# Four layer norms: three tiles by token halves instead of two, three more weight slots, subtraction on VectorE, scale on ScalarE

## Chip, cores and metric

One core of one Trainium2 chip. The metric is device time in microseconds (us) of one execution of the whole program; lower is better.

## What is computed

Two transformer blocks on 512 tokens of 1024 channels, in float32. The first has RMS norms, two kinds of attention and a feed-forward part. The second is run for two layers, and the change is all in it:

```python
def layernorm(x, g, b):
    mu = jnp.mean(x, axis=-1, keepdims=True)
    var = jnp.mean(jnp.square(x - mu), axis=-1, keepdims=True)
    return (x - mu) * lax.rsqrt(var + LN_EPS) * g + b

def hybrid_layer(x, ...):
    fq, fk, fv, f_logit, rq, rk, rv, rg = split(x @ w_in)
    fox_out = fox_attention(fq, fk, fv, log_f)      # 8 heads, causal softmax
    ret_out = silu(rg) * groupnorm(retention(...))
    mix = concat(fox_out, ret_out) @ w_out
    x = layernorm(ALPHA * x + mix, ln1_g, ln1_b)
    ff = square(relu(x @ w_ff1)) @ w_ff2            # 1024 -> 4096 -> 1024
    return layernorm(ALPHA * x + ff, ln2_g, ln2_b)
```

So there are four layer norms: after the mix and after the feed-forward part of each layer. Three are followed by more products ("inner" norms), the fourth by the output.

## The kernel before

Activations lie transposed: channels on the 128 partitions, eight tiles `H[:, j, :]` of 128x512, a column per token. Products are made in full precision out of three passes: activations and weights are each split into a high and a low part of a reduced type (`Phi`/`Plo` or `Qhi`/`Qlo`, and `wh`/`wl`), and `product` issues hi·hi, lo·hi and hi·lo (L267, L269, L270). A `gemm` makes one output tile of 128 channels: 8 products, so 24 matmuls of 512 columns, and then an evacuation out of PSUM.

**Weights.** A slab of 1 MB (or two transfers of 512 KB) is loaded by the SP queue into one of two buffers `stage` (`load_slab`). `prepare` takes the next piece, half a slab, which is what one gemm needs: ScalarE copies the high part (L239), VectorE subtracts it for the low part (L240), both 128x1024, into one of four slots `wh`/`wl` in a ring. Splitting a slab's second piece frees the buffer and issues the next load. `piece(ahead)` hands out the next piece, after it has seen to it that pieces are split `ahead` of it.

**Order.** Every engine has one queue, in the order in which this Python code calls `PE.op`, `V.op` (VectorE), `A.op` (ScalarE), `G.op` (GpSimd) and `SP.op`. An operation waits by semaphores for the ones that it is given, and all behind it in its queue wait with it. Work that is to run under the gemms is a generator in `background`. `tick()`, called after each product, adds `pace[0]` to a counter and does one background step for each whole one. The softmax heads of the attention (`softmax_heads`) are such work: for 8 heads of 4 rows the scores, the reduce (L621), the exponential (L630), the reciprocal (L635), the scaling (L640), transposes on TensorE (L647), the copy and split of what they give (L652, L653) and the product with the values (L662). They run under the gemms for queries, keys and rotary parts, at a pace of 0.46.

**A layer norm.** `Norm.tile(j)` is called once a tile j of `H` is added up. It keeps a running sum in `accq` (L1050), has an estimated centre `cB` made after tile 1, and then sums squares of deviations from that centre: subtract (L1066), square on ScalarE (L1074), add (L1082). That is done for tiles 0 to 5, whole tiles of 512 tokens. Tiles 6 and 7 are made by `last_pair`, by halves of 256 tokens (`A_`, `B_`): both tiles for half A, then both for half B. While TensorE makes half B, the mean of half A (`mean`: a matmul with ones, copied to `muB`, L1092 to L1094) and its scale (`scale`: L1104, then logarithm and exponential, L1108 and L1109) come in between. `mean` also issues the subtraction of `muB` from all eight tiles of the half, two on VectorE and six on GpSimd (L1100). Per tile follow on VectorE the multiplication by the gain and by `rB` (`gained`, L1113), on ScalarE the bias (L1119) and the copy to `Phi` (L1122), and on VectorE the low part `Plo` (L1123). With these the first two products of what comes next (`head`) start, again first half A, then half B. In an inner norm `prepare(G)` gives one weight split to GpSimd.

In the last norm of the program there is no next product. `out_half` stores the tiles by DMA as they come.

Of the kernel before, what the change touches and what calls it, by code (L numbers as in the profile page):

```python
# [93 lines left out]
def build(nc, xT, w_in, gate_up, w_bm, w_bg, w_out, w_up, w_down, w_in2, w_out2, w_ff1, w_ff2,  # L94
          consts, params, out, vrev, cneg):
    ctx = ExitStack()
    with ctx:
# [15 lines left out]
        wl = [at(f"wl{i}", 32 + 4 * i, [128, 1024], F32R) for i in range(4)]  # L113
        Phi, Plo = at("Phi", 48, [128, 8, S], F32R), at("Plo", 64, [128, 8, S], F32R)
# [97 lines left out]
        w_tok, w_free = {}, [None] * 4  # L212
        state = {"slab": 0, "prep": 0, "use": 0, "bank": 0}
# [10 lines left out]
        def prepare(low=V):  # L224
# [3 lines left out]
            state["prep"] += 1  # L228
            n, part, (k0, k1, c0, c1), last = pieces[i]
# [4 lines left out]
            if m <= 16:  # L234
                both = wh[i % 4][:, 0:8 * (32 + m)].rearrange("p (k c) -> p k c", k=8)
                hi, lo = both[:, :, 0:m], both[:, :, 32:32 + m]
            else:
                hi, lo = (w[i % 4][:, 0:size].rearrange("p (k c) -> p k c", k=k1 - k0) for w in (wh, wl))
            t_hi = A.op(lambda e: e.activation(hi, src, ACT.Copy), st_landed[n], w_free[i % 4], sem=s_whi)  # L239
            t_lo = low.op(lambda e: e.tensor_tensor(lo, src, hi.bitcast(F32), ALU.subtract),  # L240
                          st_landed[n], t_hi, w_free[i % 4], sem=s_wlo if low is V else None)
            if m <= 16:
                t_lo = [t_lo, V.op(lambda e: e.memset(both[:, :, m:32].bitcast(F32), 0.0), w_free[i % 4], sem=s_wlo)]
# [34 lines left out]
        def gemm(x, nk, evac):  # L278
# [11 lines left out]
            w_free[i % 4] = x.free = t  # L290

        def gemm_thin(x, dst, wait):
# [12 lines left out]
            w_free[i % 4] = x.free = t  # L305
# [4 lines left out]
        def gemm_pair(x, evac0, evac1, order=range(8), between=None):  # L310

            two = [(piece(), next_bank()) for _ in range(2)]
            for n, k in enumerate(order):
                for (i, w), b in two:
                    t = product(banks[b][:, :], w, k, slice(0, 128), x, k, n == 0, n == 7, free[b] if n == 0 else None)
                    if n == 7:
                        w_free[i % 4] = t
# [8 lines left out]
        def gemm_tok(x, evac):  # L326

            for q in range(4):
# [17 lines left out]
                w_free[i % 4] = t  # L346
# [629 lines left out]

        def hidden(scale_tok=None):
# [18 lines left out]
        def ff(up, first):  # L996


            for g in range(4):
                for j in range(2 if g == 0 else 0, 8):  # L1000
                    gemm(P, 8, lambda o, t, j=j: up(j, o, t))
                for j in range(6 if g == 3 else 8):
                    def ev(o, t, j=j, g=g):
# [6 lines left out]
                        return t_h[j]  # L1010
                    gemm(Q, 8, ev)
# [5 lines left out]
        for j in ff(up1, None):  # L1017
# [17 lines left out]
        class Norm:  # L1035
# [9 lines left out]
            def tile(self, j):  # L1045
# [9 lines left out]
                for k in {2: (0,), 3: (1, 2), 4: (3, 4), 5: (5,)}.get(j, ()):  # L1055
# [503 lines left out]
```

How the kernel before makes its waits and increments, by code:

```python
    def run(self, eng):  # L85
        for need, fn, s, inc in self.ops:
            for w, v in need:
                eng.wait_ge(w.h, v)
            ins = fn(eng)
            if s:
                ins.then_inc(s.h, inc)
# [1400 lines left out]
        @block.sync  # L1492
        def _(e):
            SP.run(e)
            e.wait_ge(s_out.h, s_out.n)
```

## Time and profile before

| | before |
|---|---|
| runs | 2193.04, 2193.93, 2195.63 us, median 2193.93 |
| the profiled execution | 2193.07 us |
| its span in the trace | 2191.1 us |
| mean granted TensorE clock | 0.986 of full |
| TensorE matmul (PE) busy | 2089.3 us (95%) |
| TensorE weight load (PEld) | 1702.0 us (78%) |
| VectorE (DVE) | 1120.9 us (51%) |
| ScalarE (ACT) | 924.7 us (42%) |
| GpSimd (POOL) | 189.8 us (9%) |

The profile is of one execution. PEld runs beside PE. Matmuls are pipelined: the duration of one in the trace runs from its start to its end through the array, so their starts lie closer than their durations.

### The profile page before, as it was taken

What the parts mean: (1) busy time and instruction counts of PE and PEld (TensorE: products, weight loads), DVE (VectorE), ACT (ScalarE), POOL (GpSimd) and SP (SyncE); (2) the same over time, 40 slices, a digit from 0 to 9 for tenths busy, and PEclk for the clock granted to TensorE, in tenths of its full rate; (3) what the DMA queues carried; (4) which work ended last, traced back from release to release, by engine and by line L of the source; (5) the groups of instructions that cost most, each with busy time, mean ns of one, the idle gap of its engine ahead of it and who ended that gap; (6) DMA issues with size and microseconds to landing.
All of it is one profiled execution on the core that took longest, in us unless ns stands there. A gap on an engine that the chain in (4) does not pass through costs nothing.

```text
span 2191.1 us, 24398 instructions
## 1 busy us (share of the span) xinstructions
PE 2089.3 (95%) x9592; PEld 1702.0 (78%) x9592; DVE 1120.9 (51%) x1744; ACT 924.7 (42%) x1497; POOL 189.8 (9%) x258
## 2 busy tenths in 40 slices
PE   6999999999999999999998999998999998999997
PEld 5778767888888888777787888887777677888886
DVE  4555554655433434567466333337667465333336
ACT  4565222524422323455546243343565346243343
POOL 0000000000000000243011000002353010000001
PEclk9999999999999999999999999999999999999998
DMA  6332211323223232633221223232533231323231
GB/s 210 87 92 74 77 58 58 135 92 101 96 95 98 96 96 78 183 92 97 101 96 59 96 96 96 96 96 59 164 106 92 92 96 58 96 96 96 96 96 58
DMA packets 201517, 211.36 MB, mean 96 GB/s; under 512 B 7803, under 2 KB 181115, under 8 KB 201404
## 3 DMA queue, kind: packets, MB, share of 16 engines
q1 hardware_dynamic: 194544, 194.13, 27.8%
q0 software_dynamic: 6352, 15.24, 2.7%
q8 instruction: 76, 1.25, 0.2%
q10 hardware_dynamic: 508, 0.43, 0.1%
q14 instruction: 37, 0.30, 0.0%
HBM read 194.55 MB, written 8.95 MB: 93 GB/s over the span
## 4 chain that ended last, share of the span: by engine, by line
PE 82%; DVE 8%; ACT 7%; issue 2%; DMA 0%; POOL 0%; DVEq 0%; ACTq 0%; SPq 0%
PE ps L267 23%; PE ps L270 23%; PE ps L269 23%; PE ps L335 2%; PE ps L340 2%; PE ps L338 2%; PE ps L662 1%; PE ps L647 1%; ACT H L1119 1%; PE ps L1412 1%; DVE wl L240 1%; ACT wh L239 1%; PE ps L1398 1%; ACT Phi L1122 1%; DVE d L1066 1%
## 5 line engine op out<-in xcount | busy, mean ns | idle before, releaser
L267 PE MATMUL ps<-Phi,wh 128*128 128x512 f32 (+1 forms) x1520 | 610.5, 402 | 37.3 <-DVE Plo L1123 20.4
L270 PE MATMUL ps<-Phi,wl 128*128 128x512 f32 (+1 forms) x1520 | 587.6, 387 | 0.0
L269 PE MATMUL ps<-Plo,wh 128*128 128x512 f32 (+1 forms) x1520 | 587.4, 386 | 0.0
L239 ACT ACTIVATE wh<-stage 128x1024 fp32r<-128x1024 f32 (+1 forms) x339 | 351.6, 1043 | 289.8 <-PE ps L270 278.7
L240 DVE TENSOR_TENSOR wl<-stage,wh 128x1024 fp32r<-128x1024 f32 x333 | 406.4, 1222 | 70.3 <-ACT wh L239 62.9
L267 PE MATMUL ps<-Qhi,wh 128*128 128x512 f32 (+1 forms) x1056 | 402.7, 381 | 0.8 <-DVE Qlo L400 0.8
L270 PE MATMUL ps<-Qhi,wl 128*128 128x512 f32 (+1 forms) x1056 | 399.2, 378 | 0.0
L269 PE MATMUL ps<-Qlo,wh 128*128 128x512 f32 (+1 forms) x1056 | 399.2, 378 | 0.0
L267 PEld LDWEIGHTS ps<-Phi,wh 128*128 128x128 f32 x1520 | 290.5, 191 | 104.5 <-issue 43.7
L270 PEld LDWEIGHTS ps<-Phi,wl 128*128 128x128 f32 x1520 | 290.0, 191 | 58.0
L269 PEld LDWEIGHTS ps<-Plo,wh 128*128 128x128 f32 x1520 | 290.9, 191 | 53.6 <-issue 4.1
L267 PEld LDWEIGHTS ps<-Qhi,wh 128*128 128x128 f32 x1056 | 200.9, 190 | 38.8 <-ACT Qhi L399 1.6
L269 PEld LDWEIGHTS ps<-Qlo,wh 128*128 128x128 f32 x1056 | 200.8, 190 | 37.4 <-issue 1.0
L270 PEld LDWEIGHTS ps<-Qhi,wl 128*128 128x128 f32 x1056 | 200.7, 190 | 36.4
L400 DVE TENSOR_TENSOR Qlo<-f,Qhi 128x512 fp32r<-128x512 f32 x96 | 66.5, 693 | 253.3 <-ACT Qhi L399 253.3
L1009 DVE TENSOR_TENSOR H<-H,ps 128x512 f32<-128x512 f32 x74 | 50.8, 687 | 221.1 <-PE ps L270 221.1
L985 ACT ACTIVATE rl<-ps 128x512 f32<-128x512 f32 x64 | 38.2, 598 | 194.7 <-PE ps L270 194.7
L990 ACT ACTIVATE f<-rl 128x512 f32<-128x512 f32 x96 | 60.7, 632 | 116.6 <-DVE rl L987 114.5
L335 PE MATMUL ps<-wh,Phi 128*128 128x512 f32 x224 | 92.5, 413 | 1.9 <-DVE x_rb L1351 1.9
L340 PE MATMUL ps<-wl,Phi 128*128 128x512 f32 x224 | 89.1, 398 | 0.0
L338 PE MATMUL ps<-wh,Plo 128*128 128x512 f32 x224 | 88.8, 396 | 0.0
L1310 POOL TENSOR_SCALAR x_bi<-x_Cb,stat 128x128 f32<-128x128 f32 (+1 forms) x64 | 69.3, 1083 | 116.1 <-DVE stat L621 110.1
(287 smaller groups left out, 1899.9 us busy)
## 6 DMA issues: line engine op xcount, KB each, us to landing
stage<-in_w_ff SPq DMA_DIRECT2D x64, 1024.0 KB, 5.3
stage<-in_w_in SPq DMA_DIRECT2D x39, 1024.0 KB, 5.1
stage<-in_w_up SPq DMA_DIRECT2D x16, 1024.0 KB, 5.2
stage<-in_w_down SPq DMA_DIRECT2D x16, 1024.0 KB, 5.2
stage<-in_w_in SPq DMA_DIRECT2D x30, 512.0 KB, 5.0
stage<-in_w_out SPq DMA_DIRECT2D x12, 1024.0 KB, 5.3
stage<-in_w_bg SPq DMA_DIRECT2D x4, 1024.0 KB, 5.5
vrev<-H SPq DMA_DIRECT2D x2, 2048.0 KB, 12.6
```

The costliest lines, as they stand in the source:

```text
L239: t_hi = A.op(lambda e: e.activation(hi, src, ACT.Copy), st_landed[n], w_free[i % 4], sem=s_whi)
L240: t_lo = low.op(lambda e: e.tensor_tensor(lo, src, hi.bitcast(F32), ALU.subtract), st_landed[n], t_hi, w_free[i % 4], sem=s_wlo if low is ...
L267: PE.op(lambda e: e.matmul(o, hi[:, k, c], x.hi[:, kx, tok], start=first, stop=False), t_hi, t_x or x.t[kx], list(waits), signal=False)
L269: PE.op(lambda e: e.matmul(o, hi[:, k, c], x.lo[:, kx, tok], start=False, stop=False), signal=False)
L270: return PE.op(lambda e: e.matmul(o, lo[:, k, c], x.hi[:, kx, tok], start=False, stop=last), t_lo, sem=s_wpe, signal=last)
L335: PE.op(lambda e, k=k, kk=kk, sl=sl, o=o, hi=hi: e.matmul(o, x.hi[:, kk, sl], hi[:, k, :], start=(kk == 0), stop=False), t_hi, x.t[kk], fr ...
L338: PE.op(lambda e, k=k, kk=kk, sl=sl, o=o, hi=hi: e.matmul(o, x.lo[:, kk, sl], hi[:, k, :], start=False, stop=False), signal=False)
L340: t = PE.op(lambda e, k=k, kk=kk, sl=sl, o=o, lo=lo: e.matmul(o, x.hi[:, kk, sl], lo[:, k, :], start=False, stop=(kk == 7)), t_lo, sem=s_w ...
L400: t2 = V.op(lambda e: e.tensor_tensor(lo, src, hi.bitcast(F32), ALU.subtract), t1, t_src, x.free, after)
L990: t = A.op(lambda e: e.activation(f[:, :], r[:, :], ACT.Square), t_r, f_free[j % 2])
L1009: t_h[j] = V.op(lambda e: e.tensor_tensor(H[:, j, :], H[:, j, :], o, ALU.add), t, t_h[j])
L1310: t = G.op(lambda e: e.tensor_scalar(bi[n % 2][:, 0:w], Cb[h % 2][:, 0:w], stat[:, 96 + 8 * i + h:97 + 8 * i + h], None, ALU.add), t_Cb[h] ...
```

## The change

- `last_pair` becomes `last_three`: tiles 5, 6 and 7 are made by token halves, and the next stage begins with three products by halves instead of two.
- Three more weight slots (`wxh`/`wxl`), used by `prepare(extra, room)`. `ahead_of(j)` and a further `prepare(2, ...)` split five pieces around tile 4. The extra slots lie in room that is free only then. `prepare` no longer goes to GpSimd.
- The subtraction of the mean (`minus`) is on VectorE for all eight tiles. VectorE multiplies by `rB` only (`times`); ScalarE's activation, which added the bias, now multiplies by the gain too. The order in which mean, scale and these steps are put between the products is new.
- The input stage of each layer makes query and key pair 1 before the attention's heads begin. The pieces of `w_in` are reordered for that, and the pace under which the heads run goes from 0.46 to 0.52.
- `ff` starts at tile 3 and leaves three tiles over.

```diff
+        for i, off in enumerate((54, 62, 84)):
+            wh.append(at(f"wxh{i}", 111 + off, [128, 1024], F32R))
+            wl.append(at(f"wxl{i}", 115 + off, [128, 1024], F32R))
...
             pair_cols(w_in2[L], 0)
+            pair_cols(w_in2[L], 1)
             cols(w_in2[L], 1536, 1544)
             values(w_in2[L], 1024, 1536)
-            pair_cols(w_in2[L], 1)
...
-        def prepare(low=V):
+        def prepare(extra=None, room=None):
...
+            if extra is None:
+                u = state["ring"] % 4
+                state["ring"] += 1
+            else:
+                u = 4 + extra
+                w_free[u] = room
+            slot[i] = u
...
+        def ahead_of(j):
+            if j >= 2:
+                prepare()
+            if j == 4:
+                prepare()
+                prepare(0, done(PE, V, A))
+                prepare(1, w_free[4])
...
-        def ff(up, first):
+        def ff(up, first, begun, whole):
...
-                for j in range(2 if g == 0 else 0, 8):
+                for j in range(begun if g == 0 else 0, 8):
...
-                for j in range(6 if g == 3 else 8):
+                for j in range(whole if g == 3 else 8):
...
+                    if g == 3 and whole == 5:
+                        ahead_of(j)
                     gemm(Q, 8, ev)
...
-                for k in {2: (0,), 3: (1, 2), 4: (3, 4), 5: (5,)}.get(j, ()):
+                for k in {2: (0,), 3: (1, 2), 4: (3, 4)}.get(j, ()):
...
-                for k in range(8):
-                    q = V if k < 2 else G
-                    self.d[k] = q.op(lambda e, k=k: e.tensor_tensor(d8[:, k, sl], H[:, k, sl], muB[:, sl],
-                                                                    ALU.subtract), t_m, t_h[k], self.d[k])
+            def minus(self, *ks):
+                sl = self.sl
+                for k in ks:
+                    self.y[k] = V.op(lambda e, k=k: e.tensor_tensor(d8[:, k, sl], H[:, k, sl], muB[:, sl], ALU.subtract),
+                                     self.t_m, t_h[k], self.n.d[k])
...
+            def times(self, *ks):
+                sl = self.sl
+                for k in ks:
+                    t = V.op(lambda e, k=k: e.tensor_tensor(d8[:, k, sl], d8[:, k, sl], rB[:, sl], ALU.mult),
+                             self.r, self.y[k])
+                    g, b = (prm[:, v + k:v + k + 1] for v in (self.vg, self.vb))
+                    self.fin[k] = A.op(lambda e, k=k, g=g, b=b: e.activation(H[:, k, sl], d8[:, k, sl], ACT.Identity,
+                                                                             bias=b, scale=g), t)
...
+            for p in range(3):
+                part(p, 0, range(8))
+            norm.add()
+            part(0, 1, range(3))
+            A_.mean()
+            A_.minus(0, 1, 2, 3)
+            part(0, 1, (3, 4))
+            A_.scale()
+            A_.minus(4, 5, 6, 7)
+            part(0, 1, (5, 6, 7))
+            A_.times(0, 1)
+            A_.lows(0)
+            part(1, 1, range(8))
+            for k in range(2, 5):
+                A_.times(k)
+                A_.lows(k - 1)
+            part(2, 1, range(8))
+            norm.add()
...
             if L == 0:
                 gemm_pair(P, ev_fq(0), ev_fk(0))
+                gemm(P, 8, ev_fq(1))
             else:
-                last_pair(norm, None, V_LN2G, V_LN2B, (ev_fq(0), ev_fk(0)))
+                last_three(norm, None, V_LN2G, V_LN2B, (ev_fq(0), ev_fk(0), ev_fq(1)))
                 t_ph = done(V, A, PE)
+            gemm(P, 8, ev_fk(1))
...
             gemm_tok(P, ev_fv)
-            pace[0] = 0.46
+            pace[0] = 0.52
...
-            for ev in (ev_fq(1), ev_fk(1), ev_r(0), ev_fq(2), ev_fk(2), ev_r(1), ev_r(2), ev_fq(3), ev_fk(3),
+            for ev in (ev_r(0), ev_fq(2), ev_fk(2), ev_r(1), ev_r(2), ev_fq(3), ev_fk(3),
                        ev_r(3), ev_r(4), ev_r(5), ev_r(6), ev_r(7)):
...
-            for j in range(2, 6):
+            for j in range(2, 5):
+                ahead_of(j)
                 gemm(Q, 8, ev_out(j))
-                prepare()
+                if j == 4:
+                    prepare(2, done(PE, V, A))
                 norm.tile(j)
...
-            for j in ff(up, alpha):
+            for j in ff(up, alpha, 3, 5):
```

VectorE's queue at the start of the first inner norm's stage, before. L1454 adds a whole tile into `H` (tiles 3, 4 and 5 here), L240 is a weight split, L1142 adds a half tile:

```order
L1454 SCALAR_TENSOR_TENSOR H<-H,ps 128x512
L240 TENSOR_TENSOR wl_55<-stage_50,wh_51 128x1024
L1050 TENSOR_TENSOR accq<-accq,H 128x512
L1066 TENSOR_TENSOR d_127<-H,cB 128x512 x2
L1082 TENSOR_TENSOR acc_128<-acc_128,sq_80 128x512
L1454 SCALAR_TENSOR_TENSOR H<-H,ps 128x512
L240 TENSOR_TENSOR wl_56<-stage_50,wh_52 128x1024
L1050 TENSOR_TENSOR accq<-accq,H 128x512
```

The same place now, from tile 3's sum of squares on: L250 is the weight split, L1491 adds tile 4, L1180 a half tile, and L1109 and L1087 are its sum and deviation:

```order
L1103 TENSOR_TENSOR acc_134<-acc_134,sq_85 128x512
L250 TENSOR_TENSOR wl_55<-stage_50,wh_51 128x1024
L250 TENSOR_TENSOR wl_56<-stage_50,wh_52 128x1024
L250 TENSOR_TENSOR wxl_60<-stage_49,wxh_59 128x1024
L250 TENSOR_TENSOR wxl_62<-stage_49,wxh_61 128x1024
L1491 SCALAR_TENSOR_TENSOR H<-H,ps 128x512
L250 TENSOR_TENSOR wxl_64<-stage_50,wxh_63 128x1024
L1071 TENSOR_TENSOR accq<-accq,H 128x512
L1087 TENSOR_TENSOR d_133<-H,cB 128x512 x2
L1103 TENSOR_TENSOR acc_134<-acc_134,sq_86 128x512
L1103 TENSOR_TENSOR acc_134<-acc_134,sq_85 128x512
L1180 SCALAR_TENSOR_TENSOR H<-H,ps 128x256
```

Four splits now stand ahead of tile 4's addition and a fifth right behind it, where one stood behind each tile.

ScalarE's queue in the heads of a layer, before. L556 and L571 evacuate a query and a key pair, L239 is a weight copy, and the rest are the heads' exponentials, scalings and copies:

```order
L630 ACTIVATE x_pS_145,stat<-x_pS_145,stat 128x128
L652 ACTIVATE x_PT_147<-ps 128x2x128
L556 ACTIVATE f1qs_138<-ps 64x512
L556 ACTIVATE f1qs_141<-ps 64x512
L239 ACTIVATE wh_54<-stage_49 128x1024
L640 ACTIVATE tB<-tB,stat 128x512
L630 ACTIVATE x_pS_146,stat<-x_pS_146,stat 128x256
L652 ACTIVATE x_PT_147<-ps 128x3x128
L640 ACTIVATE x_pS_145<-x_pS_145,stat 128x128
L571 ACTIVATE f1kh_139<-ps 64x512
L571 ACTIVATE f1kh_142<-ps 64x512
L239 ACTIVATE wh_51<-stage_49 128x1024
```

The heads' first rows now; L662, L650 and L640 are the former L652, L640 and L630, and L249 is the weight copy:

```order
L662 ACTIVATE x_PT_153<-ps 128x2x128
L249 ACTIVATE wh_52<-stage_50 128x1024
L650 ACTIVATE tB<-tB,stat 128x512
L640 ACTIVATE x_pS_152,stat<-x_pS_152,stat 128x256
L662 ACTIVATE x_PT_153<-ps 128x3x128
L650 ACTIVATE x_pS_151<-x_pS_151,stat 128x128
L640 ACTIVATE rB,stat<-rB,stat 128x384
L662 ACTIVATE x_PT_153<-ps 128x4x128
L650 ACTIVATE x_pS_152<-x_pS_152,stat 128x256
L566 ACTIVATE f0qs_138<-ps 64x512
L566 ACTIVATE f0qs_141<-ps 64x512
L249 ACTIVATE wh_53<-stage_50 128x1024
```

More rows of the heads stand between two weight copies than before.

## Rows read from the trace of the kernel before

**Rows 1.** Waits of PE, whole program: us in total, times, longest.

```profile
PE ps L267 <- DVE Plo L1123: 20.4, 13, 3.7
```

**Rows 2.** Stretches: us, busy (instructions) by engine, granted clock, DMA share, GB/s.

```profile
1136.60:1178.00 41.40, 30.89 (x202) 28.52 (x201) 35.61 (x64) 22.54 (x50) 12.55 (x13) 0.88 0.12 37
1178.00:1505.30 327.30, 327.30 (x1444) 270.60 (x1443) 121.26 (x135) 122.82 (x163) 0.00 (x0) 1.00 0.30 97
1505.30:1545.70 40.40, 31.02 (x201) 28.54 (x201) 34.47 (x65) 21.77 (x50) 12.54 (x13) 0.87 0.11 31
1577.00:1715.00 138.00, 131.13 (x640) 106.76 (x639) 94.58 (x203) 77.18 (x163) 51.81 (x71) 1.00 0.36 103
1792.90:1834.30 41.40, 31.19 (x202) 29.26 (x201) 35.61 (x64) 22.53 (x50) 12.55 (x13) 0.84 0.12 37
```

The columns of busy time are PE, PEld, DVE, ACT and POOL. The first, third and fifth stretch are the inner norms, the second is the feed-forward part between two of them, the fourth the softmax heads of the second layer.

**Rows 3.** Timeline of the first inner norm: start, duration, engine, line.

```profile
1140.78 0.42 DVE L1087 TENSOR_TENSOR accq<-accq,H 128x256 f32<-128x256 f32 x1
...
1143.08 2.58 POOL L240 TENSOR_TENSOR wl<-stage,wh 128x1024 fp32r<-128x1024 f32 x1 [107.31 <-DVE H L1142]
...
1143.34 2.61 DVE L1066 TENSOR_TENSOR d<-H,cB 128x256 f32<-128x256 f32 x1
...
1147.67 1.83 DVE L1100 TENSOR_TENSOR d<-H,muB 128x256 f32<-128x256 f32 x2
```

**Rows 4.** Groups by line and shape: count, busy us, mean ns, idle before.

```profile
L240 DVE TENSOR_TENSOR wl<-stage,wh 128x1024 fp32r<-128x1024 f32 x333 | 406.4, 1222 | 70.3 <-ACT wh L239 62.9 <-issue 6.6
L239 ACT ACTIVATE wh<-stage 128x1024 fp32r<-128x1024 f32 x336 | 350.8, 1050 | 289.8 <-PE ps L270 278.7 <-DMA stage<-in_w_in 7.5 <-PE ps L340 3.1
L399 ACT ACTIVATE Qhi<-f 128x512 fp32r<-128x512 f32 x96 | 60.7, 632 | 3.1
L1119 ACT ACTIVATE H<-d,prm 128x256 f32<-128x256 f32 x64 | 30.7, 496 | 3.3 <-DVE d L1113 3.1
L1122 ACT ACTIVATE Phi<-H 128x256 fp32r<-128x256 f32 x48 | 20.0, 417 | 1.5
L402 ACT ACTIVATE Phi<-H,prm 128x512 fp32r<-128x512 f32 x16 | 11.4, 716 | 25.8 <-DVE H L963 25.8
L630 ACT ACTIVATE tB<-tB,stat 128x512 f32<-128x512 f32 x16 | 11.4, 713 | 2.3 <-DVE stat L621 2.2
L653 DVE TENSOR_TENSOR x_PT<-ps,x_PT 128x512 fp32r<-128x512 f32 x16 | 11.0, 690 | 14.4 <-ACT x_PT L652 14.3
L621 DVE CUSTOM_DVE_ANT_0 tB<-ps,x_bi 128x512 f32<-128x512 f32 x16 | 10.8, 676 | 0.7 <-PE ps L618 0.5
```

**Rows 5.** Timeline of VectorE just before the first inner norm.

```profile
1131.35 0.69 DVE L1454 SCALAR_TENSOR_TENSOR H<-H,ps 128x512 f32<-128x512 f32 x1 [1.02 <-PE ps L270]
...
1135.50 0.68 DVE L1082 TENSOR_TENSOR acc<-acc,sq 128x512 f32<-128x512 f32 x1
```

**Rows 6.** DMA issues: count, KB each, median us from issue to landing.

```profile
stage<-in_w_ff SPq DMA_DIRECT2D x64, 1024.0 KB, 5.3
```

**Rows 7.** Timeline of the last norm.

```profile
2161.66 0.28 PE L267 MATMUL ps<-Qhi,wh 128*128 128x256 f32 x1
...
2161.77 0.28 PE L269 MATMUL ps<-Qlo,wh 128*128 128x256 f32 x1
...
2176.13 0.41 DVE L1146 TENSOR_TENSOR H<-H,ps 128x256 f32<-128x256 f32 x1
...
2182.72 5.09 ACT L1119 ACTIVATE H<-d,prm 128x256 f32<-128x256 f32 x12
```

**Rows 8.** Waits in the heads of the second layer, 1577 to 1715 us.

```profile
ACT x_PT L652 <- PE ps L647: 7.9, 9, 2.1
PEld ps L647 <- ACT x_PT L652: 5.3, 4, 1.6
...
PE ps L647 <- DVE stat L635: 3.0, 3, 1.2
...
PE ps L647 <- ACT tB L640: 2.1, 2, 1.2
```

More of the change, by code:

```diff
@@ L1128, in last_pair @@
-        def last_pair(norm, scale, vg, vb, nxt, out_half=None):
-            two = [(piece(3 - p), (next_bank(), 6 + p)) for p in range(2)]
-            def part(p, hf, ks):
-                sl = halves[hf]
-                (i, w), b = two[p][0], two[p][1][hf]
+                self.r = A.op(lambda e: e.activation(rB[:, sl], tB[:, sl], ACT.Exp, scale=-0.5), t, n.start)
+            def times(self, *ks):
[6 more added lines that the diff above has]
+                                                                             bias=b, scale=g), t)
+                    if self.keep:
+                        self.sub[k] = A.op(lambda e, k=k: e.activation(P.hi[:, k, sl], H[:, k, sl], ACT.Copy),
+                                           self.fin[k], P.free)
@@ new lines, in lows, with last_three, part @@
+            def lows(self, *ks):
+                sl = self.sl
+                for k in ks if self.keep else ():
+                    t = V.op(lambda e, k=k: e.tensor_tensor(P.lo[:, k, sl], H[:, k, sl], P.hi[:, k, sl].bitcast(F32),
+                                                            ALU.subtract), self.sub[k])
+                    self.sub[k] = [self.sub[k], t]
+        def last_three(norm, scale, vg, vb, nxt, out_half=None):
+            tail = [piece(1) for _ in range(3)]
+            low = [next_bank() for _ in range(3)]
+            high = [next_bank(), 6, 7]
+            A_, B_ = (Half(norm, sl, vg, vb, nxt is not None) for sl in halves)
+            def part(p, hf, ks, then=True):
+                sl, (i, w), b = halves[hf], tail[p], (low, high)[hf][p]
@@ L1166, in last_pair @@
-            part(0, 0, range(8))
-            if nxt:
-                prepare(G)
-            part(1, 0, range(8))
-            norm.add()
-            part(0, 1, range(4))
-            norm.mean(A_)
-            part(0, 1, (4, 5))
-            norm.scale(A_)
-            a = norm.r, norm.d
-            norm.d = [None] * 8
-            part(0, 1, (6, 7))
-            burst(0, *a, (0, 1, 2), (0, 1))
-            part(1, 1, range(8))
-            if nxt:
-                two = [(piece(1), next_bank()) for _ in range(2)]
@@ L1185, in head @@
+            part(2, 1, range(8))
+            norm.add()
+            if nxt:
+                two = [(piece(1), next_bank()) for _ in range(3)]
+            def head(half, ks):
                 for k in ks if nxt else ():
                     for (i, w), b in two:
[L1187 to L1191 removed]
@@ L1207, in last_pair @@
[L1207 to L1216 removed]
+                        t = product(banks[b][:, half.sl], w, k, slice(0, 128), P, k, k == 0, k == 7, free[b],
+                                    tok=half.sl, t_x=half.sub[k])
@@ new lines, in head @@
+                        if k == 7 and half is B_:
+                            P.free = t
+                return t if nxt else None
+            head(A_, (0, 1))
+            B_.mean()
+            A_.times(5)
+            A_.lows(4)
+            B_.minus(0, 1)
+            head(A_, (2, 3))
+            B_.scale()
+            A_.times(6)
+            A_.lows(5)
+            B_.minus(2, 3, 4)
+            A_.times(7)
+            A_.lows(6, 7)
+            head(A_, (4, 5, 6, 7))
+            if not nxt:
+                out_half(0, A_.fin)
```

140 lines of the change are left out of this document (54 added, 86 removed).

## The prediction

> **What bounds the kernel now.** I read the page's engine line first, then who waits for whom, then a table of stretches, and the timeline only where a stretch loses time. TensorE (PE) has matmuls in flight almost everywhere, and its waits of note stand in a few places. The largest, 20.4 us behind L1123, falls in the layer norms [rows 1]. The table shows what a norm costs: the three inner ones take 41.4, 40.4 and 41.4 us, with PE busy for 31 of them, while an undisturbed stretch of 327.3 us runs 1444 matmuls of 512 columns, 0.227 us each [rows 2]. The 192 products of 256 columns in a norm come every 0.12 us [rows 7] and fill 23 us. So each inner norm loses some 16 us, part of it at a granted clock of 0.84 to 0.88 [rows 2], which is full clock with stretches at the half level (1.2 GHz). The engine that is short there is VectorE (DVE): 35.6 busy us of 41.4.
>
> The timeline says why DVE is short. A subtraction or addition of 128x256 takes 0.42 us on its own. One that began while POOL's weight split of 2.58 us was running took 2.61 us, and two that ran beside POOL's row of subtractions took 1.83 us together [rows 3]. So an operation beside POOL costs 0.9 us instead of 0.42, and with POOL out of the norm that surcharge goes. Operations that don't wait start 0.34 us apart.
>
> **Term 1, the inner norms.** The change takes one more product (24 matmuls of 512 columns, 5.45 us) into the front of each stage and one into its back. The old cost to compare with is 41.4 + 10.9 = 52.3 us, 51.3 for the second.
>
> The new stage has 288 products of 256 columns, 34.6 us, and four statistics matmul pairs of some 0.3 us, 1.2 us. To it come the waits. I lay the first from rows, with T the start of the stage.
> - Tile 3 is added at T - 5.2 us, as [rows 5] has it for tile 4 now. Behind it on DVE stand five operations of 0.60 to 0.68 us with two short waits for the squares, until T - 1.0.
> - Then four weight splits in a row (1.22 us alone, 1.14 apart) [rows 4] until T + 3.6, and tile 4's addition until T + 4.2, though its product ended at T.
> - The fifth weight piece lies in a slab whose buffer comes free with the second of the four splits, T + 1.3. The transfer lands 5.3 us after issue [rows 6]: T + 6.7. ScalarE (ACT) copies the high part in 1.05 us, DVE subtracts until T + 8.9. DVE stands still for 3.5 us, and behind the split, in its queue, wait tile 4's sums and everything of the three half tiles.
> - Sums and deviations of tile 4: 0.6 x 3 and two of 0.7: T + 12.1. Three half tiles, 1.1 us each, and two additions of squares of 0.45 between: T + 16.1. With 0.15 us to reach PE the first mean starts at T + 16.3. PE has 81 products ahead of it, 9.7 us: it waits 6.6 us.
> - The other 207 products take 24.8 us, the statistics 1.2, ends at 42.3. Behind the first mean the old stage loses about 13 us; DVE's surcharge is gone, but ACT's is new: scale and bias both come from a column of parameters. A bias column costs 0.08 us (496 against 417 ns) and a scale column 0.08 us (716 against 632 ns) [rows 4], so the new operation takes 0.58 us against 0.50, eight times per half, in the chain to each first product. I take a bit under half of the 13, 6.1 us (between 3 and 9).
>
> That is 48.4 us, a gain of 3.9 us for the first and third norm. The second one's slab comes as two transfers, 0.4 us later, so 48.8 and a gain of 2.5 us. Together -10.3 us (ends: +1 and -19).
>
> A rule speaks to the wait for the slab. The Trainium skill (DMA: Bandwidth & Descriptors, "Anatomy of one DMA — SWDGE (gpsimd) path") fits a transfer with about 2.0 us plus its bytes over 436 GB/s, for 1 MB an estimate of 4.4 us. The trace has 5.3 us for these slabs, issued from SP. By the page the three waits would be 0.9 us shorter each and the sum 2.7 us lower, 2189.3 us; I use the row.
>
> **Term 2, the last norm.** No next product hides there. Now it takes 26.2 us from its first product to the last store into H (2161.6 to 2187.8), 31.6 with the product that the change takes in; its last half tile is added 11.7 us before that end [rows 7]. New: 144 products and two statistics, 18.1 us, 0.3 until the last addition, then 24 DVE operations of 0.34 (8.2 us, 0.7 for waits among them), and from the first multiplication with the new scale on ACT's eight at 0.49 apart, which end 10.9 us after the addition. 18.1 + 0.3 + 10.9 = 29.3, and 0.6 for what I can't see: 29.9. Gain 1.7 us (ends: 0 and 4). The output transfers behind it stay.
>
> **Term 3, the heads.** What the change takes as cover for the norm it takes from the softmax heads. Query and key pair 1 move ahead of the stretch in which the heads' steps are dealt out between products, and the pace goes from 0.46 to 0.52 steps per three matmuls (0.68 us). A row of scores is two steps: 2.96 us of cover now, 2.62 then, 0.34 us less for each of 32 rows, 10.9 us per layer, which is just the two products. A row whose chain (reduce, exponential, reciprocal, scaling, transposes, split) fits loses nothing; one that is waited for loses 0.34. Now PE's transposes wait in about nine turns of the 32: 3 for L635, 2 for L640, 4 at the weight side, and ACT waits 9 times for the transposes [rows 8]. DVE is busy for 94.6 and ACT for 77.2 of 138 us [rows 2], so nobody is full, but a denser row makes more of them wait. I take 16 of 32: +5.4 us per layer, +10.9 in both (ends: 0 and 21.8).
>
> **Edits at nothing.** The longer ff stretches: PE busy throughout [rows 2], splits hidden, two fewer products counted above. The column order of the two input slabs: both land long before use. The swap of the fused multiply (0.47 us) for a plain one (0.42) is within term 1's waits. 168 more PE instructions are the split of seven products, in the counts of 256 columns already.
>
> **Sum.** -10.3 - 1.7 + 10.9 = -1.1 us, against the profiled execution's 2193.07 us: **2192.0 us**. The median shown is 2193.93, 0.9 us above it. A measurement can tell 0.2%, 4.4 us, from no change; the forecast is no change that can be told.
>
> **Rivals.** *The heads have room* (0.28, faster). If only the nine turns that wait now lose, or if the waits behind the first mean are nearer 3 us, the result is 2193.07 - 12.0 + 6.1 = 2187.2, down to 2181.1 with heads that lose nothing. For it: DVE and ACT are idle for a third of the heads' stretch. Against: they wait for each other, not for room.
>
> *The heads' chain becomes the bound* (0.20, slower). If the chain of a row is longer than 2.62 us, every row gives back its 0.34: +21.8 - 12.0 = +9.8, 2202.9 us. It makes the kernel slower by 0.2% from 24 of 32 rows on. For it: a 512-column row has 0.68 us for the reduce (DVE), 0.71 for the exponential and about as much for the scaling (ACT), the transposes, ACT's copy and 0.69 for the split [rows 4] one after the other, more than a row's cover, and only overlap of rows hides it. Against: the short rows have a quarter to a half of those columns, and the waits now are short (ACT's nine are 7.9 us).
>
> *The norm does not profit at all*: if the idle of 6.6 us ahead of the first mean pulls the clock to its half level for longer than now (0.88 over 41.4 us is some 10 us at half), the norms' gain falls by up to 3 us each and the sum is 2201; it is in the slower 0.20.
>
> **Chances and range.** Forecast 0.52 (2188 to 2197), faster 0.28, slower 0.20. The range of 8 in 10 reaches into both neighbours: 2185 to 2199.
>
> **What would show it.** POOL without work in the norms, and DVE's 256-column operations all at 0.42 us. PE waiting once for 6 to 7 us for L1109 ahead of the first mean of each inner norm, and DVE idle 3 to 4 us before the fifth split for a copy that waits for a DMA. Stages of 48 to 49 us. More turns in which L657 (the transposes) waits, and a heads' stretch 5 to 6 us shorter per layer rather than 10.9. A first mean without that wait, or heads whose stretch shrinks by the whole 10.9, would make the forecast wrong on the fast side; a stage over 51 us or an unshortened heads' stretch on the slow side.

## The result

The changed kernel is slower: 2200.96 us median (2197.48 to 2202.06, 7 runs) against 2193.93 (2193.04 to 2195.63), ratio 1.0028, 95% interval 1.0017 to 1.004. The prediction said 2192.0 us, no change, with 2185 to 2199 as range. It missed both: the kernel got slower by more than the 0.2% that can be told, and the time lies above the range.

The page of the profiled execution of the changed kernel (2201.67 us), its first lines:

```profile
span 2199.9 us, 24753 instructions
## 1 busy us (share of the span) xinstructions
PE 2087.5 (95%) x9760; PEld 1704.1 (77%) x9760; DVE 1112.3 (51%) x1811; ACT 931.5 (42%) x1501; POOL 140.3 (6%) x207
```

POOL has lost the 50 us of work that it did in the norms, and DVE has none the more of it: 1112 us against 1121. PE is busy as long as before. The span grew in waits.

PE's waits in the whole program, changed kernel (us in total, times, longest):

```profile
PE ps L1124 <- DVE accq L1109: 26.0, 7, 7.4
...
PE ps L657 <- ACT tB L650: 11.9, 7, 2.0
...
PE ps L672 <- DVE stat L645: 8.0, 9, 1.8
PE ps L657 <- DVE stat L645: 6.7, 11, 1.1
PE ps L277 <- ACT H L1151: 4.7, 3, 1.6
...
PE ps L277 <- DVE Plo L1160: 1.9, 6, 0.4
```

The 20.4 us behind `Plo` of [rows 1] are down to 1.9. In their place PE waits 26.0 us for `accq`, the input of the first mean. And the softmax heads wait more. In the kernel before, the same view has for the second and third of these:

```profile
PE ps L647 <- ACT tB L640: 4.1, 4, 1.6
...
PE ps L662 <- DVE stat L635: 1.4, 2, 1.0
```

Stretches of the changed kernel: the three inner norms, then, in each layer, from the end of the thin product for the forget gates to the next norm (us, busy PE, PEld, DVE, ACT, POOL, clock, DMA share, GB/s):

```profile
1141.80:1191.60 49.80, 39.71 (x297) 38.25 (x296) 38.34 (x89) 26.97 (x53) 0.00 (x0) 0.93 0.13 43
1508.00:1558.20 50.20, 39.11 (x298) 37.65 (x297) 38.16 (x90) 26.33 (x54) 0.00 (x0) 0.93 0.09 22
1801.10:1850.70 49.60, 39.61 (x297) 38.16 (x297) 38.29 (x89) 27.04 (x53) 0.00 (x0) 0.93 0.14 43
...
910.10:1141.80 231.70, 216.21 (x984) 168.45 (x983) 138.35 (x275) 125.84 (x230) 58.91 (x81) 1.00 0.35 101
1567.20:1801.20 234.00, 217.28 (x985) 169.83 (x984) 139.28 (x275) 113.19 (x220) 60.05 (x83) 0.99 0.35 109
```

and the last two of these stretches in the kernel before:

```profile
897.30:1136.60 239.30, 230.48 (x1057) 182.46 (x1056) 148.79 (x287) 132.43 (x238) 61.63 (x87) 1.00 0.36 105
1549.20:1792.90 243.70, 232.10 (x1057) 183.47 (x1056) 148.71 (x288) 119.50 (x228) 63.87 (x88) 0.99 0.37 113
```

From these the balance can be drawn up. Three whole-tile products (16.35 us) left each of the two long stretches: two to the front of the layer, and tile 5 to the norm. Norms are compared as in the prediction, with 10.9 us added to the old ones.

| part | before, moved products allowed for | changed | difference |
|---|---|---|---|
| inner norms | 52.2, 51.1, 52.2 | 49.7, 50.1, 49.4 | -6.3 |
| last norm to the end | 29.4 + 5.45 = 34.9 | 32.7 | -2.1 |
| heads' stretch, first layer | 239.3 - 16.35 = 222.95 | 231.7 | +8.8 |
| heads' stretch, second layer | 243.7 - 16.35 = 227.35 | 233.9 | +6.5 |
| two feed-forward stretches | 327.5 - 10.9 = 316.6 each | 316.6 each | 0 |
| before the first norm's layer | same code | | +1.9 |

The sum is +8.8 us, the difference of the two spans. The 1.9 us in code that is the same are chance: over the profiles below that part varies by 2.5 us. The heads' stretches, too, differ by up to 2 us between profiles with the same code in them (239.3 and 241.1 us in the first layer of the kernel before and of e4). The norms repeat better, within 0.1 us in the kernel before and within 0.6 us in the changed one. With the split late (e3) they do not, as shown there. The feed-forward stretches repeat to the tenth.

### The profile page after: what moved, and what is told of

Its sections match the earlier page's. It is cut to its first block, busy times and chain, and to the rows that moved or that the text cites. A ratio compares the mean times of both kernels' runs of the same rounds, so it can differ in the third digit from the quotient of the medians.

```text
span 2199.9 us, 24753 instructions
## 1 busy us (share of the span) xinstructions
PE 2087.5 (95%) x9760; PEld 1704.1 (77%) x9760; DVE 1112.3 (51%) x1811; ACT 931.5 (42%) x1501; POOL 140.3 (6%) x207
## 4 chain that ended last, share of the span: by engine, by line
PE 40%; DVE 8%; ACT 5%; issue 3%; DMA 1%; POOL 0%; DVEq 0%; ACTq 0%; SPq 0%; POOLq 0%
PE ps L277 12%; PE ps L280 11%; PE ps L279 11%; DVE wl L250 1%; PE ps L672 1%; DVE d L1133 1%; PE ps L1449 1%; ACT H L1151 1%; PE ps L1435 1%; ACT x_PT L662 1%; ACT wh L249 1%; DMA stage<-in_w_in 0%; DMA stage<-in_w_ff 0%; PE ps L350 0%; PE ps L345 0%
## 5 line engine op out<-in xcount | busy, mean ns | idle before, releaser
L277 PE MATMUL ps<-Phi,wh 128*128 128x512 f32 x1400 | 567.7, 406 | 14.2 <-ACT sq L454 12.8
L280 PE MATMUL ps<-Phi,wl 128*128 128x512 f32 x1400 | 548.0, 391 | 0.0
L279 PE MATMUL ps<-Plo,wh 128*128 128x512 f32 x1400 | 547.6, 391 | 0.0
L249 ACT ACTIVATE wh<-stage 128x1024 fp32r<-128x1024 f32 x330 | 341.4, 1043 | 295.0 <-PE ps L280 278.5
L250 DVE TENSOR_TENSOR wl<-stage,wh 128x1024 fp32r<-128x1024 f32 x327 | 398.4, 1222 | 78.3 <-ACT wh L249 68.2
L277 PE MATMUL ps<-Qhi,wh 128*128 128x512 f32 (+1 forms) x1088 | 408.7, 376 | 0.8 <-DVE Qlo L410 0.8
L277 PEld LDWEIGHTS ps<-Phi,wh 128*128 128x128 f32 x1400 | 264.7, 189 | 76.3 <-issue 27.4
L280 PEld LDWEIGHTS ps<-Phi,wl 128*128 128x128 f32 x1400 | 263.8, 188 | 57.1
L279 PEld LDWEIGHTS ps<-Plo,wh 128*128 128x128 f32 x1400 | 264.7, 189 | 52.5 <-issue 4.1
L277 PEld LDWEIGHTS ps<-Qhi,wh 128*128 128x128 f32 x1088 | 206.8, 190 | 38.1 <-ACT Qhi L409 1.6
```

The costliest lines, as they stand in the source:

```text
L250: t_lo = V.op(lambda e: e.tensor_tensor(lo, src, hi.bitcast(F32), ALU.subtract), st_landed[n], t_hi, w_free[u], sem=s_wlo)
L277: PE.op(lambda e: e.matmul(o, hi[:, k, c], x.hi[:, kx, tok], start=first, stop=False), t_hi, t_x or x.t[kx], list(waits), signal=False)
L279: PE.op(lambda e: e.matmul(o, hi[:, k, c], x.lo[:, kx, tok], start=False, stop=False), signal=False)
L280: return PE.op(lambda e: e.matmul(o, lo[:, k, c], x.hi[:, kx, tok], start=False, stop=last), t_lo, sem=s_wpe, signal=last)
```

## The experiments

All ratios are to the kernel before, measured beside each experiment on the same chip, where its median was 2195.3 to 2196.0 us. The 2193.93 us of the result were measured apart from these, so across them the ratios count and not the medians.

**e1, the old input stages.** Pieces, order and pace of the heads as before, and only two next products behind the second norm. That norm then needs no fifth weight split, and has none. `NEW` is empty, so the lines under it are left out of the program:

```diff
+        NEW = ()
...
-                gemm(P, 8, ev_fq(1))
+                if L in NEW:
+                    gemm(P, 8, ev_fq(1))
...
-            gemm(P, 8, ev_fk(1))
+            if L in NEW:
+                gemm(P, 8, ev_fk(1))
...
-            pace[0] = 0.52
+            pace[0] = 0.52 if L in NEW else 0.46
...
-                if j == 4:
+                if j == 4 and L:
                     prepare(2, done(PE, V, A))
```

> The changed kernel with the input stages as before: query and key pair 1 are made while the softmax heads run, pace 0.46, the old order of the weight pieces, and the second norm starts two next products instead of three. All four norms keep three tiles by halves, VectorE's subtraction and ScalarE's scale. Theory 1 (the two products per layer were cover that the heads needed): the 15 us that the heads' stretches gave back come back, 2201 - 15 = 2186 us (2183 to 2189), below the kernel before. Rival (the norms are what made the kernel slower, the heads only shift where time is counted): 2199 us or more.

Measured 2186.03 us, ratio 0.9954 (0.9941 to 0.9966). The heads' stretches take 234.0 and 238.8 us, within 0.5 us the old ones less tile 5 (233.9 and 238.3). The second norm takes 42.5 us, with one product less than the 50.1 of the changed kernel (44.6), so 2.1 us of the run's gain are the missing fifth split. So the new norms without the new input stages make the kernel faster, and the new input stages turn this into a loss. But the run undoes cover and pace together, and can't say which of them it was.

**e2, pace 0.46 alone.**

```diff
-            pace[0] = 0.52
+            pace[0] = 0.46
```

> The changed kernel with only the pace of the heads at 0.46 again; query and key pair 1 stay ahead of the heads. Theory 1 (cover is what is missing, whatever the pace): the rows that no longer get their turn under products run bare at the end of the stretch, 2201 within 3 us. Rival (steps dealt out too densely are what waits): the waits of the transposes fall back to those of before and most of the 15 us come back, 2190 us or less.

Measured 2192.07 us, ratio 0.9984 (0.9975 to 0.9993). The rival is much the nearer, though the time is 2 us above its "2190 us or less", and my theory was wrong in the main: in the profiles 10 of the heads' 15 us come back by one number. The stretches:

```profile
909.20:1137.00 227.80, 216.06 (x985) 170.26 (x984) 138.30 (x275) 126.28 (x230) 60.64 (x81) 0.99 0.36 103
1562.60:1790.40 227.80, 216.12 (x985) 169.94 (x984) 138.84 (x275) 113.42 (x220) 60.36 (x83) 0.99 0.36 112
```

PE has the same work as in the changed kernel (216 us), and the stretches are 3.9 and 6.2 us shorter. What is left of the loss is 4.9 and 0.4 us: the part of cover.

**e7, pace 0.52 in the kernel before.** The same number the other way round, with no product taken away.

```diff
-            pace[0] = 0.46
+            pace[0] = 0.52
```

> The kernel before with only the pace of the heads at 0.52. No product is taken from them. Theory 1 alone (cover is what was missing in the changed kernel): the heads end earlier and nothing is lost, within 2 us of before, 2194 to 2196. Theory 2, formed from the run at 0.46 (a denser row makes more transposes wait, and that was about half of the loss): each layer's stretch loses 2.5 to 4.5 us, together 5 to 9 us slower than before, about 2202 us where before is 2196.

Measured 2210.24 us, ratio 1.0066 (1.0053 to 1.008): 14 to 15 us lost, more than either theory said. The two stretches are now

```profile
897.60:1143.30 245.70, 232.26 (x1056) 183.56 (x1055) 148.96 (x287) 132.69 (x238) 62.98 (x87) 0.99 0.36 102
1555.90:1807.00 251.10, 233.27 (x1057) 183.35 (x1056) 149.46 (x288) 119.92 (x228) 63.71 (x88) 0.99 0.38 109
```

against 239.3 and 243.7. Norms (41.27, 40.22, 41.28 us) and everything else are unchanged. In the second layer PE's waits now include these (us, times, longest):

```profile
PE ps L647 <- DVE stat L635: 4.4, 6, 2.1
PE ps L647 <- ACT tB L640: 3.2, 2, 2.0
PE ps L662 <- DVE stat L635: 3.1, 3, 1.8
PE ps L616 <- DMA f1kl<-f1kl: 2.6, 1, 2.6
```

PE waits not only at the transposes: also at the product with the values (L662), one row further down, and once for a copy by DMA of a head's keys, which now is wanted too early.

**e12 and e13, pace 0.50.** One in the kernel before, one in the changed kernel, the same edit with 0.50.

> The kernel before with the pace at 0.50 alone. If the cost of density grows evenly from 0.46 to 0.52 (+15 us): +10 us over before, 2205. If it sets in where a row's chain no longer fits under its cover, between 0.50 and 0.52, within 4 us of before, 2196 to 2199 us.

> The changed kernel with only the pace at 0.50. If the step between 0.50 and 0.52, which the kernel before has, is here too: most of the 9 us of the run at 0.46, about 2193 us where the changed kernel has 2201. If with two products less cover the cost begins earlier: 2197 us or more.

e12: 2196.22 us, ratio 1.0001 (0.9993 to 1.001). e13: 2193.05 us, ratio 0.9985 (0.9977 to 0.9994), as good as at 0.46. The stretches of e13:

```profile
907.90:1133.10 225.20, 214.57 (x985) 168.88 (x984) 139.06 (x275) 126.88 (x230) 62.31 (x81) 1.00 0.35 104
1558.30:1787.30 229.00, 216.12 (x985) 169.85 (x984) 140.24 (x275) 113.64 (x220) 61.96 (x83) 0.99 0.36 111
```

The cost isn't even over pace: it is a step between 0.50 and 0.52, in both kernels. At 0.50 a row of scores (two steps) gets exactly four products, 2.72 us. Above it some rows get three. That this count is the cause, and not another alignment that changes between 0.50 and 0.52, is my reading and wasn't tried by itself. The waits say which rows it is. In the heads' stretches of e13 (first layer, then second) PE waits for the transposes' input only like this:

```profile
PE ps L657 <- DVE stat L645: 6.3, 7, 1.8
...
PE ps L657 <- DVE stat L645: 7.6, 8, 1.9
```

Every fourth row, the widest with 512 columns, lies in `tB`. PE waits 11.9 us for it in the changed kernel and 7.1 in these two stretches of e7, and not at all in those of e13 and e12. The same holds for the product with the values, L672 and L662, behind L645 and L635: 7.0 and 4.2 us at 0.52, none at 0.50. So what the step brings in both kernels are waits for the widest rows and for the product behind them.

**e3, the fifth weight split late.** The slot is the same and it waits for the same work; only the place in the queues of ACT and DVE is another.

```diff
                 if j == 4:
-                    prepare(2, done(PE, V, A))
+                    fifth.append(done(PE, V, A))
...
             A_.minus(4, 5, 6, 7)
+            if nxt and fifth:
+                prepare(2, fifth.pop())
             part(0, 1, (5, 6, 7))
```

The timeline of VectorE in the changed kernel, start of the first inner norm, shows what it is about:

```profile
1140.93 2.36 DVE L250 TENSOR_TENSOR wl<-stage,wh 128x1024 fp32r<-128x1024 f32 x2
1143.21 2.36 DVE L250 TENSOR_TENSOR wxl<-stage,wxh 128x1024 fp32r<-128x1024 f32 x2
1145.48 0.68 DVE L1491 SCALAR_TENSOR_TENSOR H<-H,ps 128x512 f32<-128x512 f32 x1
1150.01 1.23 DVE L250 TENSOR_TENSOR wxl<-stage,wxh 128x1024 fp32r<-128x1024 f32 x1 [3.85 <-ACT wxh L249]
...
1158.15 0.42 DVE L1109 TENSOR_TENSOR accq<-accq,H 128x256 f32<-128x256 f32 x1
```

and ScalarE's and PE's rows that belong to it:

```profile
1148.86 1.06 ACT L249 ACTIVATE wxh<-stage 128x1024 fp32r<-128x1024 f32 x1 [5.18 <-DMA stage<-in_w_ff]
...
1158.63 1.22 PE L1124 MATMUL ps<-accq,onec 128*128 128x256 f32 x2 [6.93 <-DVE accq L1109]
```

VectorE stands still for 3.85 us behind ScalarE's copy, which waits for the transfer. The halves that PE had long finished are added late, the third half tile's sum at 1158.15, and PE waits 6.93 us. TensorE's clock falls to its half level (1.2 GHz) behind this wait, for some 7 us of the stage (0.93 in the mean over 49.8 us). One stretch in it:

```profile
1157.80:1161.80 4.00, 3.17 (x11) 2.81 (x12) 3.00 (x9) 1.22 (x3) 0.00 (x0) 0.50 0.00 0
```

> The changed kernel with the fifth weight split of each inner norm emitted behind the subtractions of half A instead of ahead of tile 4's sum. Theory (the split waits for a slab in flight and holds VectorE's queue, and so the first mean): PE's wait ahead of the first mean falls from 7 us to 3 or 4, and the three stages get 1.5 us shorter each, since a part comes back as waits of the first head products: 2201 - 4.5 = 2196.5 us. Rival (the norm's chain behind the first mean sets its length): the wait moves, no gain, 2200 to 2201 us.

Measured 2191.79 us, ratio 0.9982 (0.9973 to 0.9991): 9 to 10 us, twice the expected. The stages are 46.55, 47.78 and 45.99 us:

```profile
1141.70:1188.30 46.60, 39.45 (x297) 37.72 (x296) 38.27 (x89) 26.84 (x53) 0.00 (x0) 0.96 0.15 46
1504.80:1552.60 47.80, 40.70 (x297) 38.90 (x295) 38.15 (x90) 26.18 (x53) 0.00 (x0) 0.93 0.10 23
1797.60:1843.60 46.00, 37.94 (x297) 36.39 (x296) 38.14 (x89) 26.83 (x53) 0.00 (x0) 1.00 0.15 47
```

In the first, PE's wait ahead of that mean falls from 6.93 to 1.98 us, by more than the 3.85 us of standing still, since the split itself (1.23 us) is out of the way too. The granted clock of the first and third is 0.96 and 1.00 where it was 0.93, and these two gained most: 3.1 and 3.5 us against 2.3. How much of that is the clock, the later runs show, which have the same code in their first norm (e8, e11 and e14, in this order):

```profile
1133.50:1180.90 47.40, 40.66 (x297) 39.02 (x296) 38.18 (x89) 26.83 (x53) 0.00 (x0) 0.93 0.14 45
1135.60:1184.20 48.60, 41.92 (x296) 40.19 (x295) 38.14 (x89) 26.84 (x53) 0.00 (x0) 0.89 0.14 44
1136.80:1182.80 46.00, 37.93 (x296) 36.34 (x295) 38.16 (x89) 26.85 (x53) 0.00 (x0) 1.00 0.15 47
```

At the clock of the changed kernel, 0.93, the first norm takes 47.4 us here where that has 49.7, and the second takes 47.8 in e3 where that has 50.1. So the freed queue is worth some 2.3 us in each at the same clock, and what goes beyond it comes with a clock that fell less in that execution.

**e4, the kernel before with nothing on GpSimd.**

```diff
-                    q = V if k < 2 else G
+                    q = V
...
-                prepare(G)
+                prepare()
```

> The kernel before with nothing of the change but this: all eight subtractions of the mean and the weight split inside the norm are on VectorE, nothing on GpSimd. Theory (operations beside GpSimd take 0.9 us instead of 0.42): each inner norm 2 to 3 us shorter, the last 0.5 to 1 us, 2194 - 8 = 2186 us. Rival (GpSimd's twelve subtractions per norm were truly parallel, and 12 x 0.34 = 4 us more on VectorE, which is short, cost more than the surcharge): 2196 us or more.

Measured 2187.03 us, ratio 0.9958 (0.9945 to 0.997). Two lines of the change, without the rest, win 9 us; for all four norms together the prediction expected 12.0. The inner norms take 38.94, 37.91 and 38.95 us instead of 41.26, 40.22 and 41.26, which is 6.9 us in sum; the last is not shorter (29.4). DVE's busy time in the first:

```profile
1138.40:1177.50 39.10, 30.16 (x202) 27.82 (x201) 32.77 (x77) 22.68 (x50) 0.00 (x0) 0.91 0.13 41
```

13 operations more, and 32.8 us busy instead of 35.6 [rows 2].

**e5, the changed kernel with six subtractions on GpSimd.**

```diff
-                    self.y[k] = V.op(lambda e, k=k: ...
+                    self.y[k] = (V if k < 2 else G).op(lambda e, k=k: ...
```

> The changed kernel with the subtraction of the mean of tiles 2 to 7 on GpSimd again, as before; two on VectorE. Theory (what runs beside GpSimd takes about twice as long on VectorE, and the subtractions end late): each inner norm 2 to 4 us longer than the 49.7 of the changed kernel, the last 2 to 3 us, so about 11 us slower than it, 2212 us. Rival (the move is neutral here, since the norm waits for the weight slab anyway): within 2 us of 2201.

Measured 2206.72 us, ratio 1.0053 (1.0039 to 1.0066), against 1.0028 of the change. The norms are 51.85, 52.11 and 51.9 us, and the end takes 34.2 instead of 32.7. That is 8.2 us in the profile and 5.5 by the ratios, of which the intervals just touch. It is less than the 11 expected, but not the "within 2 us" of the rival.

**e6, the gain on VectorE.**

```diff
+                    t = V.op(lambda e, k=k, g=g: e.scalar_tensor_tensor(out=d8[:, k, sl], in0=d8[:, k, sl], scalar=g,
+                                                                        in1=rB[:, sl], op0=ALU.mult, op1=ALU.mult),
...
-                                                                             bias=b, scale=g), t)
+                                                                        bias=b), t)
```

> The changed kernel with the gain multiplied on VectorE together with rB, as before, and only the bias on ScalarE. Theory as predicted (the scale column costs ScalarE 0.08 us in each step of the chain to the first next product): the norms 0.2 to 0.5 us shorter each, 2200 us, hardly to be told. Rival (VectorE is what is short and the fused multiply costs it 0.05 us more): the norms longer by as much, 2202 us.

Measured 2200.0 us, ratio 1.002 (1.0011 to 1.0029): not told apart from the changed kernel. The norms are 49.39, 50.76 and 49.6. ScalarE's operation with bias alone, and, in the changed kernel, with scale and bias:

```profile
L1152 ACT ACTIVATE H<-d,prm 128x256 f32<-128x256 f32 x64 | 31.2, 502 | 12.0 <-DVE d L1149 11.5
```

```profile
L1151 ACT ACTIVATE H<-d,prm 128x256 f32<-128x256 f32 x64 | 36.9, 591 | 10.1 <-DVE d L1148 9.8
```

The scale column costs 89 ns each time, as taken. The run moves it off ScalarE and the gain onto VectorE in one go, so it shows only that the exchange as a whole costs the kernel nothing that can be seen.

**e8, old input stages and late split.** The edits of e1 and e3 together.

> The changed kernel with the old input stages (as in the first run) and the fifth weight split behind the subtractions (as in the third). If the two costs are separate, their gains add up but for the second norm, which needs no fifth split: 2186.0 - 3.1 - 3.5 = about 2179.5 us, 16 us below the kernel before. If both took the same idle time away, 2184 us or more.

Measured 2181.22 us, ratio 0.9937 (0.9925 to 0.995). This is the fastest version found, 14 us below the kernel before. It is 1.7 us above what I expected. By the ratios the two late splits are worth 3.7 us on top of e1, where 6.6 were expected, so the two gains add up only roughly here. In its profile the second norm takes 44.3 us at a clock of 0.88; in e1, with the same code there, 42.5 us at 1.00:

```profile
1497.40:1541.80 44.40, 36.73 (x249) 34.64 (x249) 36.08 (x89) 25.23 (x53) 0.00 (x0) 0.88 0.09 25
```

```profile
1498.30:1541.00 42.70, 33.94 (x249) 31.04 (x249) 35.89 (x89) 25.26 (x53) 0.00 (x0) 1.00 0.10 26
```

**e9 and e14, new order, late split, pace 0.46 and 0.44.**

> The changed kernel with the pace at 0.46 and the fifth split late; query and key pair 1 stay ahead of the heads. If pace, split and cover are three separate costs, the gains of the second and third run add up: 2201 - 9 - 9 = 2183 us, 12 to 13 us below the kernel before. If they share idle time, 2187 us or more.

> The changed kernel with the late fifth split and pace 0.44 (at 0.46: 2183.8 us). If the 5 us that the stretches still lose at 0.46 are density too: 2 to 4 us faster, 2181. If they are cover (rows left over at the end of a stretch that is two products short): 2 us slower or more, 2186.

e9: 2183.84 us, ratio 0.9946 (0.9933 to 0.9958). Pace and split are separate costs: the sum of the two gains was to give 2183 us. e14: 2185.99 us, ratio 0.9956 (0.9943 to 0.997). A smaller pace gives nothing more, so what is left is not density.

**e10 and e11, the version of e8 at pace 0.44 and 0.48.**

> The old input stages and the late fifth split (as in the eighth run, 2181 us), pace of the heads 0.44. If a thinner row is always worth something, 1 to 3 us faster, 2179. If 0.46 is the balance between rows that wait and rows that are left over bare at the end, 3 to 6 us slower, 2185 us.

> The same as the run before this, with pace 0.48. By the seventh run (0.06 more costs 15 us), if the cost grows evenly, 5 us slower than 2181, 2186 us. If the cost depends on how rows and products happen to line up, anything from 2178 to 2190, without order between 0.44, 0.46 and 0.48.

e10: 2184.89 us, ratio 0.9952 (0.9938 to 0.9966); e11: 2184.28 us, ratio 0.9949 (0.9937 to 0.9962). Both are 3 to 4 us above the 0.46 of e8 by the medians, but the intervals overlap. Within 0.44 to 0.48 the pace is worth 4 us at most, and with no order that these runs could show.

## Why the prediction failed

**Term 3 (heads) is the step that failed first.** It priced the change by cover: 0.34 us for each of 16 waiting rows in a layer, 10.9 us for both. Measured are 15.3 us. The stretches, which were to be 5 to 6 us shorter per layer, got 2.1 and 4.3 us shorter (233.85 and 238.25 without tile 5, against 231.7 and 233.9). The mechanism was wrong too. The argument treated pace and cover as one thing, since moving two products away and dealing the steps out faster go together. They are two: at 0.50 or 0.46 three quarters and two thirds of the loss are gone (e13, e2) with the same products missing, and at 0.52 the kernel before loses nearly as much, 13.8 us in these stretches, without any missing (e7). The two don't simply add up, though: 13.8 for pace and 4 to 5 for cover are more than the 15.3 of both. The linear price per row also hid the step between 0.50 and 0.52 (e12). What cover costs by itself is 4 to 5 us for both layers (3.9 in e13, 5.3 in e2), under half of what I took. The rival "the heads' chain becomes the bound" stood at 0.20, with 21.8 us and 2202.9 as its time, and is nearest to the outcome among those that blame the heads. Its condition, a chain longer than 2.62 us, is the right kind of condition, but it holds at a pace that the change need not have had, and not every row gave back its 0.34 us.

The rival "the norm does not profit at all" named 2201 us, the measured time, and that is luck. It let the norms lose up to 9 us of their gain to the clock. The clock did fall to half behind the wait of 6.93 us, but the mean over a norm rose, from 0.84 to 0.88 [rows 2] to 0.93, and the inner norms gained 6.3 us.

**Term 1 (inner norms) had the mechanisms right and the sum 4 us too good.** Expected were 48.4, 48.8 and 48.4 us; the stages took 49.7, 50.1 and 49.4. The wait for the slab came where it was laid: VectorE stood still 3.85 us (3.5 expected), the first mean waited 6.93 us in the first norm (6.6 expected) and 7.4 in the second (7.0, with the later slab). It started 16.8, 17.3 and 16.7 us into the stage instead of 16.3, 16.7 and 16.3, which is some 0.5 us of the error in each. The term "6.1 us behind the first mean", which I chose as a bit under half of the old 13, was 6.8 to 6.9 (49.7 - 16.8 - 26.0 in the first): 0.7 us more in each. The "old 13" itself was misread. Before, the first mean started 7.2 us into the first norm, just after its 60 products, so all of the loss stood behind it: 17.0 us.

**What I didn't see: where the norms' gain comes from.** I had it as one result of cover, engine and order. The runs separate it. Moving work off GpSimd gives 7 us in the old structure (e4, inner norms; subtractions and weight split together) and 8 in the new (e5, subtractions alone, with the last norm). Three tiles instead of two, with the new order that goes with them, gave nothing as built: 38.94 + 10.9 = 49.8 us without GpSimd in the old structure, 49.7 in the new. The lost time of the first norm (stage less 0.12 us for each product and 1.2 for the statistics), ahead of the first mean and behind it, says why:

| run | first mean at | lost ahead of it | lost behind it |
|---|---|---|---|
| before | 7.2 | 0.0 | 17.0 |
| e4, nothing on GpSimd | 8.5 | 1.3 | 13.4 |
| changed kernel | 16.8 | 7.1 | 6.9 |
| e3, fifth split late | 11.85 | 2.1 | 8.7 |

The three tiles win 6.5 us behind the mean, and the fifth split, which they need, costs 5.8 ahead of it. With the split late their gain is there: 3.3, 1.0 and 3.9 us in the three norms of e3, against e4. Over the six profiles with the late split the first norm takes 46.0 to 48.6 us, so the 3.3 there can be anything from 1.2 to 3.8. I knew that wait to within half a microsecond and used it as a term only, without asking what the norm would be without it.

**Term 2 (last norm)** was 1.7 us forecast, 2.1 measured. It comes from the three tiles and the new order: without GpSimd alone the last norm stays at 29.4 us (e4). **The edits at nothing** were nothing: the feed-forward stretches are shorter by 10.9 us to the tenth, and the exchange of the fused multiply can't be seen (e6).

**The transfer.** The Trainium skill (DMA: Bandwidth & Descriptors, "Anatomy of one DMA — SWDGE (gpsimd) path") gives an estimate of 4.4 us for 1 MB, by a fit for transfers issued from GpSimd. These are issued from SP. In the changed kernel ScalarE's copy began 5.5 us after the split that freed the buffer had ended (about 1143.3 to 1148.86), so the row's 5.3 us was the one to take, and the term based on it held.

Sum by the prediction's steps: -6.3 - 2.1 + 15.3 = +6.9 us, without the 1.9 us of chance ahead of the first norm; the medians differ by 7.0. Of the error of 9 us, 4.4 are the heads, 4.0 the inner norms, 0.9 is that the profiled execution lay under the median, and the last norm gives 0.4 back.

**Open.** How the cost of cover is shared by the layers (4.9 and 0.4 us in e2, 2.3 and 1.6 in e13) can't be read, since stretches with the same code differ by up to 2 us. What is called cover here is all that the new input stages do at the same pace; the moved products and the new order of the pieces were not tried apart. Open is also whether the step at 0.50 is the count of products per row.

## What to carry to other kernels

Where a change makes two edits that seem to be one (work moved away, and the rate of the rest raised to match), test each alone: here one number, which could have stayed as it was, cost 9 to 10 us and turned a gain into a loss. When a working prediction contains an operation that waits in a queue for a transfer, ask at once what stands behind it and whether it could stand later; moving it was worth another 8 to 10 us over three norms (e3, e9). And an engine that "helps" can cost more than its work: two lines that took GpSimd out of the norms gave 0.42% by themselves.

## What the runs showed of the hardware

The price of working beside GpSimd was larger than its count of operations suggests. With 13 operations more on VectorE, its busy time in a norm went down by 2.8 us (e4). In the changed kernel its 128x256 subtractions take 418 ns each, where the same operation took 948 ns in the mean beside GpSimd:

```profile
L1133 DVE TENSOR_TENSOR d<-H,muB 128x256 f32<-128x256 f32 x64 | 23.1, 418 | 0.0
```

```profile
L1100 DVE TENSOR_TENSOR d<-H,muB 128x256 f32<-128x256 f32 x16 | 14.6, 948 | 0.0
```

The Trainium skill ("SBUF — State Buffer", section "SBUF: two separate sides") says of the port pair that VectorE shares with GpSimd that whoever starts first has it for the whole instruction and the other waits, when VectorE's operation has two inputs in SBUF and GpSimd's reads SBUF. These are such operations. The traces agree: the operation beside a split of 2.58 us on GpSimd took 2.61 us [rows 3], and two that alternate with GpSimd's subtractions (873 ns in the mean) take 0.9 us each.

The granted clock of TensorE is not fixed by the code of a stage: the second norm of e1 and of e8 has the same instructions, and ran at 1.00 and 0.88, 1.8 us apart. The first norm with the late split ran at 0.89 to 1.00 in six profiles and took 48.6 down to 46.0 us. Single stages can thus differ by 2 to 3 us between two profiles, and the ratios over many runs decide.
